# Bias rows written 16 times to HBM instead of 128, and the skewed tables read back 16 partitions at a time on the SP queue

## The reference

```python
def hybrid_mixer(x, w_in, b_in, sinks, w_a, w_b, w_c, w_out, rel_bias):
    proj = x @ w_in + b_in                      # 1024 -> 6916 columns
    qa, ka, va, qb, kb, vb, qc, kc, vc, fc, gates = jnp.split(proj, SPLIT_POINTS, axis=-1)
    o_a = dilated_attention(...)   # 3 groups x 4 heads, dilation 1, 4, 16, relative bias per head
    o_b = window_gqa_with_sinks(...)   # 8 query heads, window 128, relative bias per head
    o_c = forgetting_attention(...)    # 4 heads, no table
    return merged_by_gates(o_a, o_b, o_c) @ w_out

def reference(x, mem, ...):
    x = layer_norm(ALPHA * x + hybrid_mixer(x, ...), ln1_g, ln1_b)
    x = layer_norm(ALPHA * x + memory_cross_attention(x, mem, ...), ln2_g, ln2_b)
    return layer_norm(ALPHA * x + swiglu(x, w_ffn_in, w_ffn_out), ln3_g, ln3_b)
```

## Time and profile before

| what | value |
|---|---|
| median of 3 runs | 967.56 us (967.15 to 967.98) |
| profiled execution, first to last instruction (span) | 966.1 us |
| PE busy in the span | 910.4 us, 94% |
| DVE, ACT, POOL busy | 445.2, 297.4, 85.4 us |
| mean granted TensorE clock | 0.974 |
| DMA queue of SP (q1) | 66511 packets, 86.82 MB |
| DMA queue of POOL (q0) | 3104 packets, 5.52 MB |

### The profile page before, as it was taken

One profiled execution on the slowest core, in us unless ns is written; L12 is line 12 of the kernel. 1 busy time (PEld: TensorE's weight loads), 2 busy tenths in 40 slices (PEclk: granted clock), 3 DMA queues, 4 the chain that ended last, 5 costly groups with the idle time before them and its releaser, 6 DMA issues.

```text
span 966.1 us, 11584 instructions
## 1 busy us (share of the span) xinstructions
PE 910.4 (94%) x4511; PEld 752.2 (78%) x4511; DVE 445.2 (46%) x843; ACT 297.4 (31%) x552; POOL 85.4 (9%) x123
## 2 busy tenths in 40 slices
PE   7924999999998999999999988999999999999997
PEld 7923889977855888888878968988888888888885
DVE  3211355566986252525375868333343433322244
ACT  3100214622774322222241564222222222112221
POOL 4100400007242000000002002000000000000001
PEclk9967999999999999999999999999999999999998
DMA  7683523122100222233550511122332224222221
GB/s 251 127 120 69 174 78 105 39 89 88 43 1 1 87 88 88 87 98 115 220 194 26 174 44 37 52 87 87 115 102 87 87 89 164 95 88 88 89 108 65
DMA packets 69655, 92.88 MB, mean 96 GB/s; under 512 B 3761, under 2 KB 60391, under 8 KB 69615
## 3 DMA queue, kind: packets, MB, share of 16 engines
q1 hardware_dynamic: 66511, 86.82, 26.7%
q0 software_dynamic: 3104, 5.52, 4.2%
HBM read 86.81 MB, written 5.49 MB: 96 GB/s over the span
## 4 chain that ended last, share of the span: by engine, by line
PE 86%; DMA 5%; DVE 4%; another core or an unknown queue 2%; ACT 1%; issue 1%; POOL 1%; SPq 0%; DVEq 0%; POOLq 0%; ACTq 0%
PE ps L1550 25%; PE ps L1551 25%; PE ps L1552 25%; DMA raw<-in_w_in 4%; PE ps L1669 3%; PE ps L1719 2%; PE ps L1693 1%; DMA x_nat<-in_x 1%; PE ps L1587 1%; PE ps L1992 1%; DVE w_lo L1031 1%; DVE prob L1158 1%; PE ps L1993 1%; PE ps L1994 1%
## 5 line engine op out<-in xcount | busy, mean ns | idle before, releaser
L1550 PE MATMUL ps<-xt_hi,w_hi 128*128 128x512 f32 (+1 forms) x712 | 277.3, 389 | 33.0 <-DVE w_lo L1031 30.6
L1551 PE MATMUL ps<-xt_hi,w_lo 128*128 128x512 f32 (+1 forms) x712 | 276.0, 388 | 0.0
L1552 PE MATMUL ps<-xt_lo,w_hi 128*128 128x512 f32 (+1 forms) x712 | 275.8, 387 | 0.0
L1550 PEld LDWEIGHTS ps<-xt_hi,w_hi 128*128 128x128 f32 x712 | 135.5, 190 | 61.6 <-DVE w_lo L1031 31.8
L1552 PEld LDWEIGHTS ps<-xt_lo,w_hi 128*128 128x128 f32 x712 | 135.5, 190 | 27.2
L1551 PEld LDWEIGHTS ps<-xt_hi,w_lo 128*128 128x128 f32 x712 | 135.7, 191 | 26.5
L1031 DVE TENSOR_TENSOR w_lo<-raw,w_hi 128x1024 fp32r<-128x1024 f32 (+1 forms) x59 | 71.3, 1210 | 134.4 <-ACT w_hi L767 132.1
L767 ACT CAST w_hi<-raw 128x1024 fp32r<-128x1024 f32 (+1 forms) x59 | 60.7, 1035 | 230.1 <-PE ps L1552 164.3
L1506 DVE TENSOR_TENSOR w_lo<-raw,w_hi 128x1024 fp32r<-128x1024 f32 x40 | 48.9, 1222 | 79.1 <-ACT w_hi L990 79.1
L1322 DVE TENSOR_TENSOR w_lo<-raw,w_hi 128x1024 fp32r<-128x1024 f32 x30 | 36.7, 1223 | 92.0 <-ACT w_hi L916 92.0
L990 ACT CAST w_hi<-raw 128x1024 fp32r<-128x1024 f32 x40 | 41.9, 1047 | 78.6 <-PE ps L1552 78.6
(11 more groups left out here) (248 smaller groups left out, 1354.4 us busy)
## 6 DMA issues: line engine op xcount, KB each, us to landing
raw<-in_w_in SPq DMA_DIRECT2D x25, 1024.0 KB, 5.0
raw<-in_w_ffn_in SPq DMA_DIRECT2D x22, 1024.0 KB, 5.0
raw<-in_w_ffn_out SPq DMA_DIRECT2D x11, 1024.0 KB, 4.8
raw<-in_w_mix_out SPq DMA_DIRECT2D x4, 1024.0 KB, 4.9
x_nat<-in_x SPq DMA_DIRECT2D x4, 512.0 KB, 4.8
raw<-in_w_branch_b SPq DMA_DIRECT2D x4, 512.0 KB, 4.0
resid<-in_x SPq DMA_DIRECT2D x1, 2048.0 KB, 9.8
raw<-in_w_xkv SPq DMA_DIRECT2D x2, 1024.0 KB, 6.3
```

Source lines behind the costliest of these rows:

```text
L1550: pe.matmul(dst, a_hi, b_hi, start=start, stop=False)
L1551: pe.matmul(dst, a_lo, b_hi, start=False, stop=False)
L1552: return pe.matmul(dst, a_hi, b_lo, start=False, stop=stop)
```

## The change

HBM gets 16 copies of each row instead of 128. A table is then read in eight blocks of 16 partitions: the block of partitions a to a + 15 starts a places further left and uses the same 16 copies, and one DMA covers all heads of the group. So the reads are 24 DMAs for what branch A needs (`tab1` heads 0 to 3, `tab4`, `tab16`) and 8 for branch B (`tab1` heads 4 to 11), in place of one a head. The number of bytes read stays the same. They are issued by SP instead of POOL: the 24 between chunks 7 and 8, behind waits for the four writes and for `mem_turned`, and the 8 between chunks 9 and 10. DVE waits for the first 24 where it waited for all, and for the other 8 ahead of `pt_drain(1)`.

```diff
--- before.py
+++ after.py
@@ -65,7 +65,12 @@
 SEG1, SEG4, SEG16 = 3 * P - 1, 2 * P - 1, 2 * P - 1
 SEG_N = SEG1 + SEG4 + SEG16
 PT_SLOTS = 4
+TAB_A_AFTER, TAB_B_AFTER = 7, 9
 SEG_CUT = 448
+
+ROW_COPIES = 16
+N_TAB_A = 3 * (P // ROW_COPIES)
+N_TAB_ALL = N_TAB_A + P // ROW_COPIES
 
 
 def t5_bucket(dist):
@@ -282,9 +287,9 @@
     w_f1 = A["w_ffn_in"][0].rearrange("(k p) n -> p k n", p=P)
     w_f2 = A["w_ffn_out"][0].rearrange("(k p) n -> p k n", p=P)
 
-    rows1 = nc.dram_tensor("rows1", (N_AH + N_BH, P, SEG1), F32, kind="Internal")
-    rows4 = nc.dram_tensor("rows4", (N_AH, P, SEG4), F32, kind="Internal")
-    rows16 = nc.dram_tensor("rows16", (N_AH, P, SEG16), F32, kind="Internal")
+    rows1 = nc.dram_tensor("rows1", (N_AH + N_BH, ROW_COPIES, SEG1), F32, kind="Internal")
+    rows4 = nc.dram_tensor("rows4", (N_AH, ROW_COPIES, SEG4), F32, kind="Internal")
+    rows16 = nc.dram_tensor("rows16", (N_AH, ROW_COPIES, SEG16), F32, kind="Internal")
 
     with ExitStack() as ctx:
         def sem(name):
@@ -625,8 +630,24 @@
                              (bv[:, 896:1156], A["b_in"][0:1, VC0:VC0 + 260].to_broadcast([P, 260])),
                              (sink[:, :], A["attn_sinks"][0:1, :].to_broadcast([P, N_BH]))):
                 sp.dma_start(dst, src).then_inc(small_in, 16)
+            def tables(tab, rows, h0, nh, width, cols):
+
+                for a in range(0, P, ROW_COPIES):
+                    src = bass.AP(rows, h0 * ROW_COPIES * width + P - 1 - a,
+                                  [[width - 1, ROW_COPIES], [ROW_COPIES * width, nh], [1, cols]])
+                    sp.dma_start(tab[a:a + ROW_COPIES, h0:h0 + nh, :], src).then_inc(table_in, 16)
+
             for c in range(2, CG):
                 load(c)
+                if c == TAB_A_AFTER:
+
+                    sp.wait_ge(seg_out, 16 * 4)
+                    sp.wait_ge(mem_turned, 4)
+                    tables(tab1, rows1, 0, N_AH, SEG1, 256)
+                    tables(tab4, rows4, 0, N_AH, SEG4, P)
+                    tables(tab16, rows16, 0, N_AH, SEG16, P)
+                if c == TAB_B_AFTER:
+                    tables(tab1, rows1, N_AH, N_BH, SEG1, 256)
                 if c == 3:
                     sp.dma_start(mem_nat[:, :, :], A["mem"][0].rearrange("(m p) n -> p m n", p=P)).then_inc(mem_in, 16)
 
@@ -706,13 +727,7 @@
                       (rows4, 0, N_AH, N_AH, SEG1, SEG4), (rows16, 0, 2 * N_AH, N_AH, SEG1 + SEG4, SEG16))
             for rows, to, h0, nh, at, width in copies:
                 pool.dma_start(rows.ap()[to:to + nh, :, :],
-                               seg_row[h0:h0 + nh, at:at + width].unsqueeze(1).broadcast_to([nh, P, width])).then_inc(seg_out, 16)
-            pool.wait_ge(seg_out, 16 * len(copies))
-            pool.wait_ge(mem_turned, 4)
-            for tab, rows, nh, width, cols in ((tab1, rows1, N_AH + N_BH, SEG1, 256), (tab4, rows4, N_AH, SEG4, P),
-                                               (tab16, rows16, N_AH, SEG16, P)):
-                for h in range(nh):
-                    pool.dma_start(tab[:, h, :], bass.AP(rows, h * P * width + P - 1, [[width - 1, P], [1, cols]])).then_inc(table_in, 16)
+                               seg_row[h0:h0 + nh, at:at + width].unsqueeze(1).broadcast_to([nh, ROW_COPIES, width])).then_inc(seg_out, 16)
 
             def scale_probs(j):
                 for v, f in scale_units(j):
@@ -1216,7 +1231,7 @@
                         at = (slice(None), slice(4 * hf, 4 * hf + 4), slice(m * P, (m + 1) * P))
                         dve.tensor_tensor(memt_lo[at], ps[:, 2 + n, :].rearrange("p (k c) -> p k c", k=4),
                                           f32(memt_hi[at]), ALU.subtract).then_inc(mem_lo, 1)
-            dve.wait_ge(table_in, 16 * (N_AH + N_BH + 2 * N_AH))
+            dve.wait_ge(table_in, 16 * N_TAB_A)
             for what, n in front_for_splitters():
                 if what == "split":
                     rest_of(n)
@@ -1285,6 +1300,7 @@
 
 
 
+            dve.wait_ge(table_in, 16 * N_TAB_ALL)
             pt_drain(1)
             for i in range(N_GROUP_PAIRS + 1):
                 for m in accs_ended[2 * i - 2] if i else []:
```

## The result

The changed kernel takes 933.19 us (median of 4 runs, 932.29 to 934.82), against 967.77 us for the kernel before (4 runs, 967.15 to 969.96). The earlier table has the first three of those four. The ratio is 0.9642, with a 95% interval of 0.9631 to 0.9654, so 34.6 us are gained. 932.7 was forecast. The profiled execution has a span of 933.1 us, the longest of the four (930.6 to 933.1).

The account below looks back on a forecast made before the run. PE was taken to wait for weight chunks 3 and 4, held up in the DMA queues by the row writes. 34.9 us for the writes and 0 for the rest took 967.56 to 932.7 us; range 930.5 to 941.

Parts of the forecast that it names:

- What bounds the kernel: PE waits twice, 30.0 us in all, for weights of chunks 3 and 4, held up in DMA queues by row writes.
- The writes, 34.9 us: Pieces 6 to 9 on PE: 56.7 us shrinks to 21.8 if chunks 3 and 4 land in time, gaining 34.9 us.
- the clock part (4.9 us): The part of the 34.9 us gain beyond 30.0 us of waiting, from PE's slow clock around the holes.
- the signs of being right: Chunks 3 and 4 land within 5 to 13 us, row writes within 10; PE's early waits gone, clock 1.00.
- The reads, 0: Table reads on SP's queue: 24 issues take 11.3 us within 21.9 us of cover, 8 take 3.8; cost 0.
- the prediction's sign: On SP, chunk 8 is issued less than 2 us later than its old place less 34.9 us.
- The cover: Time on SP from 112.1 to 134.0 us, the latest harmless issue of chunk 8: 21.9 us.
- Rival B: Block reads on SP outlast their cover at 1.09 us an issue, chunk 8 4.3 us late: 938 us, chance 0.12.
- Rival A: Writes shrink less than their bytes; excess of chunks 3 and 4 only halves, 12.3 us lost: 945 us, chance 0.08.
- The tail on four engines: From 82.0 to 94.1 us, DMA share 0.24: a four-head write sits on four engines, chunk 4's shares behind it.
- Rivals C and D: C: block reads run on one engine each, 1025 us, chance 0.03; D: writes not the cause, 967.6 us, chance 0.02.

Follow-up runs that it names:

- spread_heads: The kernel before, still 128 copies, with the 20 heads of the row buffer six partitions apart instead of side by side: 933.27 us, ratio 0.9638.
- split4: The kernel before, still 128 copies, with each of the four row writes cut in four along the copies: 988.95 us, ratio 1.0217.
- copies8: The changed kernel with 8 copies and blocks of 8 partitions, 48 and 16 reads: 933.79 us, ratio 0.9646.
- issues48: The changed kernel with each block read cut in two by heads, 48 and 16 reads, same bytes: 935.63 us, ratio 0.9667.
- copies64: The changed kernel with 64 copies and blocks of 64 partitions, 6 and 2 reads: 947.76 us, ratio 0.9791.

## Why the prediction was right

**What bounds the kernel.** Right. PE's two waits ended with two late loads. Both went with the slow writes, with fewer copies (the changed kernel) and with all 128 copies read from partitions further apart (spread_heads).

**The writes, 34.9 us.** Measured: 34.6 us between the medians. In the profiled executions the transposes of `mem_nat` come 106.92 - 73.56 = 33.4 us sooner. 1.3 us of the difference lie at the start of the kernel, where the matmuls of line 1629, which make the bias rows, begin at 28.01 in this execution, and the same ones in before (line 1613) at 26.71. From the first matmul of piece 6 at 51.62 to the transposes it is 21.9 us, where 21.8 was forecast for four pieces. So the clock part (4.9 us) came back as counted, and the clock is 1.00 from 20 to 120 us. Chunk 3 was forecast to land within 12.4 us of its issue and took 9.5. The row writes were forecast at up to 7.4 us, and under 10 among the signs of being right, and took 10.3: they shrank to 1/5.7, not 1/8. This did not reach PE, since chunk 3, which landed at 40.9, might have come 8 us later.

**The reads, 0.** Right for the reason given. 24 issues took 11.44 us (11.3 forecast). Chunk 8 was issued at 90.29, which is 1.6 us behind its old place of 122.01 - 33.4 (1.4 forecast). Measured as the prediction's sign has it, from 122.01 - 34.9, it is 3.2 us late and not under 2, and 1.3 us of this is the later start. The 8 later issues took 4.42 us (3.8 forecast). The cover is 21.5 us by two runs (21.9 forecast). Branch A's first reader is at 125.05, long after. Rival B's price for an issue, 1.09 us, was more than twice the 0.48 us measured. The 104 GB/s that the Trainium skill gives for partitions 0 to 15 (page "SBUF — State Buffer", section on the DMA port swizzle) could not be seen here: the 24 issues take 11.44 us, more than the 10.1 us estimated from it, which makes 92 GB/s on the whole.

**Rival A.** Its total for half the writes was 12.3 us, and 14.6 were measured with 64 copies, but that is luck, since the parts are wrong. It halved the excess of both loads. Chunk 4's did about halve (45.2 to 19.2 us), but chunk 3's went only from 30.7 to 25.3. So the first hole was 12.5 us instead of 2.7, and it hid the whole lateness of chunk 4, for which 7.7 us of hole had been worked out. The same step understated chunk 3 at 32 copies by 3 us (15.7 against 12.7), a size at which the time hides it.

**The tail on four engines.** The count of four fits the share of 0.25, and the conclusion was too narrow. "0.238 us of engine time a packet" was a price paid for waiting on one group of source partitions, not the engines' own: it fell to 0.090 with the sources spread. The rate of an undisturbed load packet (0.049 us) could not show this. For this change it made no difference, because fewer copies cut both. For split4 it made the difference between 953 and 989 us.

**Rivals C and D** did not occur. The 24 reads went by at their issue rate, and with chunk 3 and `mem_nat` still on the queue together (9.5 and 12.1 us to landing) PE waited for neither.

## What to carry to other kernels

When a load is late, look at what the DMA engines move in that time and not only at how busy they are: engines that were nine tenths busy at 27 GB/s (split4) waited for something else. A broadcast out of four neighbouring partitions was such a case here. Fewer bytes cured it, and so did sources further apart in SBUF; cutting it into more DMAs made the other loads later. Issues on a queue that waits for a buffer anyway were free up to the last moment of the load behind them, and that moment was worked out from the rows of before to half a us (21.9 against 21.5).

## What was not expected

- Four neighbouring source partitions gave 24 GB/s with a quarter of the engines' time and 25 GB/s with nine tenths of it. With heads six partitions apart, a packet of the same writes fell from 0.238 to 0.090 us.
- A load that met the slow writes could keep nearly its whole delay when their bytes were halved (chunk 3, 30.7 to 25.3 us), and it landed with the last of them.
- The issue time of a table read on SP went with its shape. The first fence is of copies8 (8 partitions), the second of issues48 (16 partitions, half the heads), the third of copies64 (64 partitions): ns, min/median/max.

```profile
L638 SPq DMA_DIRECT2D tab<-rows x64: 264/302/1814, 77.5 to 107.1; - x64
```

```profile
L640 SPq DMA_DIRECT2D tab<-rows x64: 303/423/1403, 78.0 to 111.0; - x64
```

```profile
L638 SPq DMA_DIRECT2D tab<-rows x8: 586/630/1201, 90.6 to 113.3; - x8
```
